# Sparse-attention trunk: four blocks' keys chosen inside the sparse attention, four instead of six in the latent stage

## What is computed

```python
isc = jax.nn.relu(jnp.einsum('bqhd,bsd->bqhs', qib, k_idx).astype(jnp.float32))
isc = jnp.einsum('bqh,bqhs->bqs', wib.astype(jnp.float32), isc) * idx_scale
isc = jnp.where(admissible[None], isc, -jnp.inf)
top_val, top_idx = lax.top_k(isc, top_k)
sel_ok = jnp.isfinite(top_val)
...
s = s - slopes[None, None, :, None] * dist[:, :, None, :]
s = jnp.where(sel_ok[:, :, None, :], s, -jnp.inf)
p = jax.nn.softmax(s, axis=-1)
```

## Time and profile before

| | |
|---|---|
| median of three runs | 3579.91 us (3579.02 to 3581.82) |
| the profiled execution | 3573.17 us |
| its span, first to last instruction | 3571.4 us |
| granted TensorE clock, mean | 0.971 |
| PE busy | 3304.3 us (93%) |
| DVE busy | 2058.9 us (58%) |
| ACT busy | 1910.5 us (53%) |
| POOL busy | 833.0 us (23%) |

### The profile page before, as it was taken

The page is one execution under the profiler, slowest core; times in us unless marked ns, Lnnn a source line. Parts: engine busy times, 40 slices in busy tenths (PEclk is TensorE's granted clock), DMA queues, the critical chain, the costliest instruction groups (busy, mean ns, idle before and its releaser), DMA issues. The chain is left out here.

```text
span 3571.4 us, 90235 instructions
## 1 busy us (share of the span) xinstructions
PE 3304.3 (93%) x36861; PEld 2904.3 (81%) x36861; DVE 2058.9 (58%) x4738; ACT 1910.5 (53%) x3804; POOL 833.0 (23%) x948
## 2 busy tenths in 40 slices
PE   5899999989999999997988999998689999999899
PEld 5677899988888887876766898897678888888787
DVE  7100100008799984331299998995877777777322
ACT  5122211116688883221487877745468888888311
POOL 3122200001288880001103523522410000000000
PEclk9999999989999999998998999999899999999999
DMA  5333322139623314347222436426653333331432
GB/s 200 110 113 114 135 86 67 49 80 223 166 71 86 86 43 165 124 149 225 89 59 71 148 95 189 136 83 198 213 160 86 86 86 88 95 86 52 157 115 87
DMA packets 368043, 416.92 MB, mean 117 GB/s; under 512 B 51744, under 2 KB 272800, under 8 KB 366368
## 3 DMA queue, kind: packets, MB, share of 16 engines
q1 hardware_dynamic: 302880, 318.55, 30.9%
q10 hardware_dynamic: 64768, 92.81, 7.2%
HBM read 247.21 MB, written 164.10 MB: 115 GB/s over the span
## 5 line engine op out<-in xcount | busy, mean ns | idle before, releaser
L1435 PE MATMUL s_o<-s_v,s_pT 128*64 128x65 f32 (+1 forms) x13056 | 439.8, 224 | 10.9 <-issue 8.0
L230 PE MATMUL s_acc<-s_wh,s_hT 128*128 128x256 f32 (+1 forms) x1408 | 431.3, 306 | 3.5 <-ACT s_parts L661 1.9
L232 PE MATMUL s_acc<-s_wh,s_hT 128*128 128x256 f32 (+1 forms) x1408 | 430.5, 306 | 0.0
L231 PE MATMUL s_acc<-s_wl,s_hT 128*128 128x256 f32 (+1 forms) x1408 | 429.8, 305 | 0.0
L1435 PEld LDWEIGHTS s_o<-s_v,s_pT 128*64 128x64 f32 x13056 | 404.4, 138 | 29.5 <-issue 9.4
L230 PE MATMUL s_acc<-s_hT,s_wh 128*128 128x512 f32 x880 | 351.0, 399 | 56.1 <-DVE s_wl L334 26.7
L1598 ACT ACTIVATE s_probs<-s_probs,s_nmx 128x512 f32<-128x512 f32 (+3 forms) x640 | 388.7, 661 | 12.0 <-DVE s_nmx L1663 12.0
L1647 DVE CUSTOM_DVE_ANT_0 s_probs<-s_s,s_scores 128x512 f32<-128x512 f32 (+3 forms) x640 | 364.7, 607 | 9.3 <-issue 5.4
L2426 DVE TENSOR_SCALAR_CACHE_REDUCE s_scratch<-s_scores,s_cand 128x384 uint8<-128x384 f32 (+4 forms) x320 | 365.3, 1209 | 1.1
L231 PE MATMUL s_acc<-s_hT,s_wh 128*128 128x512 f32 x880 | 348.2, 396 | 0.0
L232 PE MATMUL s_acc<-s_hT,s_wl 128*128 128x512 f32 x880 | 347.9, 395 | 0.0
(11 more groups left out here) (295 smaller groups left out, 7095.1 us busy)
## 6 DMA issues: line engine op xcount, KB each, us to landing
fm<-s_parts ACTq DMA_DIRECT2D x120, 512.0 KB, 2.8
s_y<-y SPq DMA_DIRECT2D x32, 640.0 KB, 5.9
y<-s_g SPq DMA_DIRECT2D x18, 1024.0 KB, 5.9
s_q<-fm SPq DMA_DIRECT2D x32, 512.0 KB, 6.8
kc<-s_parts SPq DMA_DIRECT2D x32, 512.0 KB, 3.1
s_w<-in_o_fm SPq DMA_DIRECT2D x25, 512.0 KB, 4.4
s_w<-in_o_w_in SPq DMA_DIRECT2D x12, 1024.0 KB, 5.4
s_qh<-fm SPq DMA_DIRECT2D x42, 256.0 KB, 3.4
```

Of the source, the lines that this page charges most:

```text
L230: nc.tensor.matmul(out, sh, mh, start=(j == 0), stop=False)
L231: nc.tensor.matmul(out, sh, ml, start=False, stop=False)
L232: ins = nc.tensor.matmul(out, sl, mh, start=False, stop=(j == n - 1))
L1435: last = nc.tensor.matmul(o_ps[half * HD:(half + 1) * HD, 0:w], pT[half][:, x0:x0 + HD], v[:, g.u.kbs[g.a + x], vc:vc + w], start=(g.first ...
```

## The change

`EARLY` goes from 8 to 10 and `LEFT` = (2, 6) names four blocks, n = 2 to 5 (b = 4 to 7, 640 to 1024 columns), that `search_all` passes over: it copies their thresholds and rooms to a small tile `kept` (`leave`) and chooses n = 0, 1, 6, 7, 8, 9. The latent stage is left with n = 10 to 13, two pairs. The four passed over are chosen within the sparse attention by `LeftChoice`, one after another, 7 down to 4, by the same six steps, with the `FirstTiles` as scratch. Two more steps make the distances for 1024 columns, from an iota that POOL writes as its first instruction of the stage. These 26 steps are dealt to the first twelve batches of pair 0, two or three at the end of each; the first use of block 7 as a bias is in the batch after. SP waits for `chosen` before it loads the `FirstTiles`.

```diff
-def sparse_attention(nc, c, fm, kc, vc, gc, y, scores, ahead, tiles):
+def sparse_attention(nc, c, fm, kc, vc, gc, y, scores, ahead, tiles, left):
...
+    due_at = min(g.u.end - g.u.ng + 1 for g in gs if g.u.j == 0 and g.u.b in left.BLOCKS) - 1 - LEAD
+    shares_of = due_at // BATCH
...
+                sp.wait_ge(chosen, 1)
                 tiles.load_weights(sp)
...
             @block.gpsimd
             def _(pool):
+                left.ramp().then_inc(ramp_made, 1)
                 for h in range(C_HEADS):
                     ins = nc.gpsimd.memset(neg_slope[:, h:h + 1], -slope[h])
...
+                def choose_left(share):
+                    if share >= shares_of:
+                        return
+                    if share == 0:
+                        dve.wait_ge(ramp_made, 1)
+                    for k in range(share * left.STEPS // shares_of, (share + 1) * left.STEPS // shares_of):
+                        if k < left.STEPS - 1:
+                            link(left.step(k))
+                        else:
+                            left.step(k).then_inc(chosen, 1)
+                            dve.wait_ge(chosen, 1)
+
...
                     bias(n + LEAD + 2)
                     bias(n + LEAD + 3)
+                    choose_left(n // BATCH)
...
-    EARLY = 8
+    EARLY = 10
+    LEFT = (2, 6)
...
+    def leave(self, dve, kept):
+
+        (first, last), v = self.LEFT, self.nc.vector
+        w = last - first
+        v.tensor_copy(kept[:, 0:w], self.thr[:, first:last])
+        self.link(dve, v.tensor_copy(kept[:, w:2 * w].bitcast(F32), self.room[:, first:last]))
+
...
+class LeftChoice:
+
+
+    BLOCKS = tuple(n + Search.B0 for n in reversed(range(*Search.LEFT)))
+    PARTS = 6
+    STEPS = 2 + PARTS * len(BLOCKS)
+
+    def __init__(self, nc, scores, kept, tiles):
+        self.nc, self.scores, self.kept = nc, scores, kept
+        self.dist, self.even, self.rank = (t[:, 0:PIECE] for t in (tiles.y, *tiles.w))
+
+    def ramp(self):
+        return self.nc.gpsimd.iota(self.dist.bitcast(I32), pattern=[[-1, PIECE]], base=PIECE - P, channel_multiplier=1)
...
+        if k == 0:
+            return v.tensor_copy(dist, dist.bitcast(I32))
+        if k == 1:
+            return v.scalar_tensor_tensor(out=dist, in0=dist, scalar=-1.0, in1=dist, op0=ALU.mult, op1=ALU.min)
...
+        if part == 0:
+            return v.tensor_scalar(ev, sc_b, t, None, ALU.is_equal)
+        if part == 1:
+            return v.tensor_tensor_scan(out=rk, data0=ev, data1=ev, initial=0.0, op0=ALU.add, op1=ALU.max)
+        if part == 2:
+            return v.tensor_scalar(room, rk[:, L - 1:L], room, 0.5, ALU.add, ALU.mult)
+        if part == 3:
+            return v.tensor_scalar(rk, rk, room, 2.0 ** -126, ALU.is_gt, ALU.mult)
+        if part == 4:
+            return v.scalar_tensor_tensor(out=ev, in0=sc_b, scalar=t, in1=rk, op0=ALU.subtract, op1=ALU.is_lt)
+        return v.scalar_tensor_tensor(out=sc_b, in0=ev, scalar=MASKED, in1=dist[:, PIECE - L:PIECE], op0=ALU.mult,
+                                      op1=ALU.add)
...
                     search.adjust(dve, 0, search.EARLY)
-                    for n in range(search.EARLY):
+                    search.leave(dve, kept)
+                    first, last = search.LEFT
+                    for n in (*range(first), *range(last, search.EARLY)):
...
+            left = LeftChoice(nc, scores, kept, tiles)
+            sparse_attention(nc, c, fm1, kc, vc, gc, y1, scores, ahead, tiles, left)
```

More of the change, by code:

```diff
@@ L1491, in sparse_attention @@
         drained = sc.sem("drained")
+        ramp_made = sc.sem("ramp_made")
+        chosen = sc.sem("chosen")
         out_made = sc.sem("out_made")
@@ L2590, in choose_two, with step @@
             self.links += 2
+class LeftChoice:
[7 more added lines that the diff above has]
+        return self.nc.gpsimd.iota(self.dist.bitcast(I32), pattern=[[-1, PIECE]], base=PIECE - P, channel_multiplier=1)
+    def step(self, k):
+        v, dist = self.nc.vector, self.dist
+        if k == 0:
+            return v.tensor_copy(dist, dist.bitcast(I32))
+        if k == 1:
+            return v.scalar_tensor_tensor(out=dist, in0=dist, scalar=-1.0, in1=dist, op0=ALU.mult, op1=ALU.min)
+        b, part = self.BLOCKS[(k - 2) // self.PARTS], (k - 2) % self.PARTS
+        L, at, w = (b + 1) * P, b - Search.B0 - Search.LEFT[0], len(self.BLOCKS)
+        t, room = self.kept[:, at:at + 1].bitcast(F32), self.kept[:, w + at:w + at + 1].bitcast(F32)
+        sc_b, ev, rk = self.scores(b), self.even[:, 0:L], self.rank[:, 0:L]
+        if part == 0:
[10 more added lines that the diff above has]
+                                      op1=ALU.add)
 class FirstTiles:
@@ L2980, in trunk @@
             all_scores = sc.sb("scores", [P, P * (NT * (NT + 1) // 2)])
+            kept = sc.sb("kept", [P, 2 * (Search.LEFT[1] - Search.LEFT[0])], U32)
             def scores(b):
@@ L3032, in trunk @@
             tiles = FirstTiles(nc, first, y1, a["o_w_out"][0], side="right")
-            sparse_attention(nc, c, fm1, kc, vc, gc, y1, scores, ahead, tiles)
+            left = LeftChoice(nc, scores, kept, tiles)
+            sparse_attention(nc, c, fm1, kc, vc, gc, y1, scores, ahead, tiles, left)
         out_project(nc, c, y1, a["o_w_out"][0], h1, a["final_norm"].rearrange("(a n) -> a n", a=1), tiles, out=out[0])
```

## The result

| | before | changed |
|---|---|---|
| median of 20 runs each | 3574.53 us | 3582.20 us |
| ratio, 95% interval | | 1.0017 (1.0009 to 1.0025), so 6.1 us slower (3.2 to 8.9) |
| profiled execution, its span | 3573.17, 3571.4 us | 3584.04, 3582.2 us |
| granted TensorE clock, mean | 0.971 | 0.970 |
| PE, DVE busy | 3304.3, 2058.9 us | 3316.0, 2059.1 us |

The forecast was 6.8 us slower. By the ratio 6.1 us were measured; the two medians lie 7.7 apart. The forecast also held that a difference of this size can't be told from none, and the interval tells it. The time before that the forecast starts from, 3579.91 us, is the median of three of these twenty runs, 5.4 above the median of all, so its 3586.7 us lies above the 3582.20 measured for that reason.

What follows compares the result with a forecast made beforehand. PE was taken to bound the sparse attention, DVE to close the latent stage. Terms 0 - 8.2 + 15.0 = +6.8 us on the median 3579.91 gave 3586.7 us, 0.19% slower; range 3581 to 3592 us.

Steps and rivals of the forecast that it cites:

- End of the input projection, 0: DVE ends there 5.9 us later at most, at 2429.4, still ahead of the last store at 2431.66: no cost.
- Latent stage, -8.2: One pair fewer: DVE no longer closes the stage, the last key store does; next stage's first load 8.2 us earlier.
- it keeps its 27.62 us: Latent stage: the pair of 1664 and 1792 columns takes as long as before, low parts included.
- The first rival: Latent stage: low parts come later still, delaying PE's last group; net +7.2 to +12 us, slower; chance 0.42.
- Pair 0, +15.0: Sparse attention: 24.8 us of steps, less 9.6 of DVE idle and 0.4 of slack, plus 0.2 for POOL's iota.
- DVE's idle 9.6 us: Pair 0, first twelve batches: DVE's idle time stands just ahead of its copies and hides 9.6 us of the steps.
- a granted clock below 1.00 in pair 0: Sign of being wrong; the rival that PE's clock falls there had up to 3635 us and chance 0.02.
- POOL's 3.3 us: Pair 0: POOL's 3.31 us busy might hold up DVE's steps, making the sum +10.1; kept as upper end, not taken.
- the 0.2%: Whole kernel: 7.2 us, the smallest difference a measurement was said to tell from no change; forecast 0.19% slower.
- the forecast's own case of +1 to +7.2: Whole kernel: net change between +1 and +7.2 us, within 0.2%; chance 0.46.
- half of 12.2 - 8.2: Range's low end: half the extra latent gain granted if the last low parts were as early as before, 12.2 us less.
- the gain of 6.6: Range's high end: latent gain remaining if the pair of 1664 and 1792 columns is as slow per column as the removed pair.

Runs made afterwards that it cites:

- Five profiles with three pairs: Profiles of kernels keeping three latent-stage pairs (the kernel before, with or without an unused tile, or sparse-attention choosing alone): latent stage 134.4 to 137.4 us.
- five with two pairs: Profiles of the changed kernel and variants with two latent-stage pairs, low parts late, no blocks chosen ahead of them: latent stage 127.7 to 129.9 us.
- the window without steps: Pair 0 window of the changed kernel with the 26 steps removed from the sparse attention: 48.67 us; whole kernel 3561.5 us, 0.9969 of the kernel before.
- the nine: Profiles of kernels whose later tiles are moved by 32 or 96 bytes per partition: 559.6 to 562.4 us behind pair 0.
- the eight: Profiles of kernels whose later tiles are moved by 0 or 64 bytes per partition: 563.0 to 566.1 us behind pair 0.
- the 24 steps: Against the kernel before, the four blocks' steps moved to DVE's waits at the latent stage's head, none in sparse attention: 3571.2 us, ratio 0.9991.

## Why the prediction was right in size and wrong in class

- **End of the input projection, 0: right.** DVE ended at 2427.4 (2429.4 at most).
- **Latent stage, -8.2: too large by 1.3 to 1.9.** Five profiles with three pairs have a mean of 135.9 us, five with two pairs 129.0: -6.9. Counted from the first pair's start, free of the scatter ahead, it is 80.4 and 74.1: -6.3. The mechanism was right, PE's last group late, 7.32 us of wait for 3.21. The step that was off is "it keeps its 27.62 us": the pair took 28.64, and PE waited 0.63 us for its low parts too. Another 0.8 us came behind PE's last group, most of it in ACT's key copies. The first rival held in this, in small.
- **Pair 0, +15.0: nearly right, +15.35 and +16.7,** by errors that cancel, so in part by luck. The step that failed is the reading that DVE's idle 9.6 us "stand just ahead of its copies": 6.9 do, and each batch hides only its own. Against this the 26 steps took 23.9 us and not 24.8, since block times worked out from starts hold the gaps between steps, and the estimate that follows, 17.0, is higher than what was measured. Nor was the loss all of the kind forecast: PE stands for 11.1 us more, not 14.8, and the rest is that it is busy for 4.3 and 5.7 us more than in the window without steps, in part at the lower clock. The prediction had a granted clock below 1.00 in pair 0 as a sign of being wrong, and it came, at 0.97 and 0.95; its waits were not 1.2 us in each batch but up to 2.81, since the steps differ in length. (The slack of 0.4 us is 0.48 by its rows.)
- **POOL's 3.3 us: nothing, as taken.** L2648 took 2.29 us on 1024 columns, as the same step of the input projection. POOL has six products in the stretch, and each ended 0.29 us or more ahead of the next step (2665.89 to 2666.62 and 2667.29, for one). By the rule of the Trainium skill (SBUF — State Buffer, Who interferes with whom) the sum was to be +10.1; there was nothing here for it to act on.
- **Missing: the new tile's place, -2.3 to -3.4** (the two profiles; the means of the nine and the eight). The change adds `kept`, which was priced by two copies alone. So -6.3 to -6.9, + 15.35 to 16.7, - 2.3 to 3.4 give some +5 to +8, against 6.1 measured. That the forecast's 6.8 is so near owes something to luck too: the latent gain was put 1.3 to 1.9 too high, and the missing term gives 2.3 to 3.4.
- **The class: wrong.** The step that failed is the 0.2% "that a measurement of this kernel can tell from no change", for which the prediction shows no working. Twenty runs of each kernel gave an interval of 0.08% to either side, 2.9 us, though single runs of one kernel spread over 16 us. With 2.9 us as the bound, most of the forecast's own case of +1 to +7.2, and all of the first rival's, would have been slower.
- **The range** has a slip at its low end: 8.2 and half of 12.2 - 8.2 are 10.2, not 9.9. At the high end it takes the gain of 6.6 and not the 5 named as the lower end. The measured value lies well within either way.

## What to carry to other kernels

Work goes where an engine waits for something that the bound's chain doesn't need next, not between two halves of the bound's batch. DVE at the head of the latent stage is the nearest to such a place here, and even there the 24 steps cost some 4 us. Between the halves of a batch each batch hides only its own gap, and a store of idle time read from a window is not to be had: a window's idle time holds the gaps between instructions, so count only what stands ahead of the instruction that will be late. A change that adds a tile moves the tiles behind it: give the kernel before the same tile, unused, ahead of reading a difference of 0.1 to 0.4% as the change's own.

## What was not expected of the hardware

- 32 bytes of tile ahead of the others made this kernel 5.0 us faster (1.8 to 8.6), 64 bytes 13.6 us (8.6 to 18.6), with the same instructions: PE's unnamed waits behind pair 0 went from 7.8 and 6.6 us to 5.6 in the first, matmuls of the input projection from 281 ns to 276 in the second, at the same granted clock. Why is not known; which tile must move was not tried.
- In two profiles of one kernel PE waited 2.81 us at the same place; the windows at its end and behind it have a mean granted clock of 0.70 and 0.73 in one, 1.00 in the other. Behind the next wait, of 2.07 us, it fell in both.
